# Two-block transformer on one core: convolution and decays made inside the projections, masks later, norms rearranged

## The reference

```python
# first block, delta rule branch
qkv = silu(centred_depthwise_conv(concatenate([q, k, v]), conv_w))   # 4 taps, 1536 channels
q, k = l2norm(heads(q)), l2norm(heads(k))
g = -exp(a_log) * softplus(a + dt_bias); beta = sigmoid(b)
o = gated_delta_rule(q, k, v, g, beta)                               # both directions

# every norm of the second block
h = rms_norm(x, norm_g) * (1.0 + scale) + shift                      # shift, scale, gate = silu(c) @ ada_w + ada_b

# second block, recurrence
q, f, i, g = split(h @ w_in)
log_f = logaddexp(log(lb), log1p(-lb) + log_sigmoid(f));  k = -expm1(log_f)
cum = cumsum(log_f)                                                  # in chunks
attn = einsum(q, k, exp(cum_t - cum_s)) for s <= t
o = attn @ i + (q * exp(cum)) @ state
```

## Time and profile before

| stretch | from, to us | PE busy | DVE busy | ACT busy | granted clock | GB/s |
|---|---|---|---|---|---|---|
| setup, to ScalarE's last copy and on | 0 to 15.3 | 0.59 | 0 | 1.92 | 1.00 | 282, then 401 |
| first norm | 15.3 to 23.2 | 7.63 | 4.37 | 3.51 | 1.00 | 388 |
| first projection, end of it | 73.0 to 81.0 | 7.22 | 2.33 | 0.39 | 0.59 | 88 |
| inputs stage, most of it | 81.0 to 111.0 | 21.25 | 20.10 | 20.44 | 0.83 | 336 |
| second projection, end | 1835.0 to 1851.6 | 15.73 | 1.62 | 1.84 | 1.00 | 253 |
| decay stage | 1851.6 to 1860.0 | 6.17 | 3.13 | 6.08 | 1.00 | 214 |
| decay stage, rest | 1860.0 to 1872.8 | 9.00 | 7.81 | 5.61 | 1.00 | 353 |
| scores, middle | 1880.0 to 1890.0 | 5.86 | 10.00 | 7.57 | 1.00 | 2 |
| scores, middle | 1890.0 to 1900.0 | 9.17 | 10.00 | 6.00 | 0.83 | 1 |

### The profile page before, as it was taken

The page is one execution under the profiler, slowest core; times in us unless marked ns, Lnnn a source line. Parts: engine busy times, 40 slices in busy tenths (PEclk is TensorE's granted clock), DMA queues, the critical chain, the costliest instruction groups (busy, mean ns, idle before and its releaser), DMA issues. The chain is left out here.

```text
span 2315.3 us, 27695 instructions
## 1 busy us (share of the span) xinstructions
PE 2050.6 (89%) x10647; PEld 1357.7 (59%) x10647; DVE 1398.4 (60%) x2485; ACT 618.2 (27%) x1042; POOL 504.8 (22%) x463
## 2 busy tenths in 40 slices
PE   7889998997997777877789888999999978899998
PEld 6679897774542222222238655666767866566684
DVE  5455563557888888655565564433757586533394
ACT  1411102422111111000020352333741061333472
POOL 1032000104443433344411170000101041100000
PEclk9889999999999999999999898999999999999999
DMA  5830655539999999999956303889995532698897
GB/s 200 308 124 1 212 192 185 218 107 411 394 421 422 421 422 421 422 421 417 422 208 208 126 2 138 358 353 361 385 388 203 198 110 75 232 368 349 351 418 275
DMA packets 142430, 650.96 MB, mean 281 GB/s; under 512 B 17975, under 2 KB 22735, under 8 KB 97083
## 3 DMA queue, kind: packets, MB, share of 16 engines
q1 hardware_dynamic: 94012, 354.09, 40.3%
q0 software_dynamic: 46336, 291.93, 30.9%
q10 hardware_dynamic: 1952, 3.18, 0.5%
HBM read 642.46 MB, written 16.85 MB: 285 GB/s over the span
## 5 line engine op out<-in xcount | busy, mean ns | idle before, releaser
L1842 PE MATMUL psum<-peer_uv_rows,peer_weight_diagonal 128*128 128x512 f32 x932 | 453.5, 615 | 109.4 <-DVE peer_weight_diagonal L1968 109.1
L1842 PEld LDWEIGHTS psum<-peer_uv_rows,peer_weight_diagonal 128*128 128x128 f32 x932 | 161.8, 190 | 391.8 <-DVE peer_weight_diagonal L1968 266.4
L1975 DVE SCALAR_TENSOR_TENSOR peer_uv_rows<-peer_uv_rows,peer_x 128x1024 f32<-128x1024 f32 x233 | 285.5, 1225 | 143.5 <-DMA peer_uv_rows<-peer_uv,peer_index 141.3
L1796 POOL DMA_INDIRECT peer_uv_rows<-peer_uv,peer_index x233 | 242.4, 1041 | 447.8 <-PE psum L1842 332.8
L147 DVE TENSOR_TENSOR moe_weight_parts<-weight_ring,moe_weight_parts 128x2048 fp32r<-128x2048 f32 x80 | 182.6, 2290 | 154.3 <-ACT moe_weight_parts L2891 153.9
L1875 ACT ACTIVATE peer_gelu<-peer_dots 128x1 f32<-128x1 f32 x256 | 51.5, 202 | 550.7 <-DVE peer_uv_rows L1975 499.1
L2891 ACT ACTIVATE moe_weight_parts<-weight_ring 128x2048 fp32r<-128x2048 f32 x80 | 152.1, 1911 | 36.7 <-DMA weight_ring<-moe_w 23.7
L153 PE MATMUL psum<-moe_weight_parts,moe_block_x_parts 128*128 128x512 f32 x352 | 142.9, 406 | 9.9 <-DVE moe_block_x_parts L147 5.3
L3010 POOL DMA_INDIRECT h_t<-moe_tokens,moe_block_tokens x30 | 35.1, 1170 | 500.4 <-PE psum L2709 410.8
L154 PE MATMUL psum<-moe_weight_parts,moe_block_x_parts 128*128 128x512 f32 x352 | 139.6, 397 | 0.0
L155 PE MATMUL psum<-moe_weight_parts,moe_block_x_parts 128*128 128x512 f32 x352 | 139.4, 396 | 0.0
(11 more groups left out here) (568 smaller groups left out, 3893.7 us busy)
## 6 DMA issues: line engine op xcount, KB each, us to landing
weight_ring<-moe_w SPq DMA_DIRECT2D x76, 2048.0 KB, 10.1
weight_ring<-ada_w SPq DMA_DIRECT2D x24, 2048.0 KB, 9.1
moe_weight_ring_end<-moe_w SPq DMA_DIRECT2D x20, 2048.0 KB, 12.6
weight_ring<-w_in SPq DMA_DIRECT2D x17, 2048.0 KB, 9.6
weight_ring<-hgrn_w_in SPq DMA_DIRECT2D x8, 2048.0 KB, 8.9
moe_results<-moe_block_out POOLq DMA_DIRECT2D x26, 512.0 KB, 9.0
weight_ring<-nsa_w_in SPq DMA_DIRECT2D x5, 2048.0 KB, 9.3
weight_ring<-peer_wq SPq DMA_DIRECT2D x4, 2048.0 KB, 8.0
```

What stands on the lines that cost most here:

```text
L1796: nc.gpsimd.indirect_dma_start(buffer(t), None, S.dram["peer_uv"], bass.IndirectOffsetOnAxis(ap=experts[:, t:t + 1], axis=0)).then_inc(row ...
L1842: last = nc.tensor.matmul(S.ps[:, 2 * a + c, :], diag[:, t % 4, :], v_rows(t)[:, c * BANK:(c + 1) * BANK], start=(i == 0), stop=(i == PICK ...
L1975: nc.vector.scalar_tensor_tensor(u_rows(t), u_rows(t), 1.0, x2[:, t // PICKS, :], ALU.mult, ALU.mult, accum_out=dots[:, t:t + 1]).then_inc ...
```

## The change

- Setup: SyncE waits only for x. The masks are loaded in the inputs stage, and so is the wait for the gate biases. The flip matrix is no longer loaded, VectorE makes it in the sparse attention.
- First projection: a class `Convolution` makes taps, SiLU and squares of q and k beside the units. The inputs stage begins with the sums of squares and v's SiLU; the six conditioning blocks come after.
- Norms with conditioning: shift and gain are made on GpSimd; VectorE evicts by column; no filler products ahead of a router, whose products wait column by column.
- Recurrence: f is projected first. A class `Decays` makes sigmoids (ScalarE), affine and floor (GpSimd), one logarithm, and the running sum as 16 scans (VectorE) beside the projection. `hgrn_decays` goes. Its three conditioning blocks are put between TensorE's levels of `hgrn_scores`, with one bank instead of two; the levels' ring is six banks; ScalarE makes the two last exponentials after level 3.

```diff
 @block.sync   # setup
                 S.w.load(sp, 1)
-                sp.dma_start(S.cst[:, C_LU:C_W], D_["cst"][:, C_LU:C_W]).then_inc(masks_in, 16)
-                S.w.load(sp, SLOTS)
                 sp.wait_ge(x_in, 16)
-                sp.wait_ge(masks_in, 16)
...
 # Conditioning.tensor
-            if i >= 2:
-                pe.wait_ge(self.moved, i - 1)
+            ahead = len(set(self.banks))
+            if i >= ahead:
+                pe.wait_ge(self.moved, i - ahead + 1)
...
 # norm_stage
+            @block.gpsimd
+            def _(pool):
+                if ada is not None:
+                    nc.gpsimd.tensor_tensor(mod[:, :], S.ada_cols[:, ada, :], S.col[:, COL_ADA + ada * 24:COL_ADA + ada * 24 + 2 * KD], ALU.add).then_inc(modulated, 1)
...
-                if ada is not None:
-                    link(nc.vector.tensor_tensor(mod[:, :], S.ada_cols[:, ada, :], S.col[:, COL_ADA + ada * 24:COL_ADA + ada * 24 + 2 * KD], ALU.add))
...
+                        for k in range(4):
+                            nc.vector.tensor_scalar(S.hT[:, k, a * P:(a + 1) * P], S.ps[:, 2 * a, k * P:(k + 1) * P],
+                                                    gain[:, k:k + 1], shift[:, k:k + 1], ALU.mult, ALU.add).then_inc(moved, 1)
...
-                    if work is None:
+                    if work is None and router is None:
                         idle_products(S, 6, 2)
...
-                            if k == 0:
-                                pe.wait_ge(moved, a + 1)
+                            if k < 4:
+                                pe.wait_ge(moved, 4 * a + k + 1)
...
+class Convolution:
+    AT = {0: (0,), 1: (1,), 4: (2, 3), 5: (4,), 6: (5,)}
...
+    def unit(self, dve, u):
+        dve.wait_ge(self.padded, 2)
+        dve.wait_ge(self.moved[u % 2], u // 2 + 1)
+        for tap in range(4):
+            for c in (2 * u, 2 * u + 1):
...
+    def scalar(self, act, i):
+        half = {4: 0, 7: 1}.get(i)
...
+        act.activation(part[:, :, :], part[:, :, :], ACT.Silu).then_inc(self.activated, 1)
...
+        act.activation(self.sq[:, 4 * half:4 * half + 4, :], part[:, :, :], ACT.Square).then_inc(self.squared, 1)
...
 # deltanet_inputs, TensorE
+                for half in range(2):
+                    for bank in range(2 * half, 2 * half + 2):
+                        last = nc.tensor.matmul(S.ps[:, bank, :], S.cst[:, C_ONES:C_ONES + P],
...
                 pe.wait_ge(cond_made, 1)
-                work.tensor(pe, 0, 3)
+                pe.wait_ge(S.bias_in, 4 * 16)
+                work.tensor(pe, 0, 2)
...
+                work.tensor(pe, 2, 6)
...
 # nsa_attention
+                nc.vector.tensor_copy(flip, ident[:, ::-1]).then_inc(flip_made, 1)
...
+                pe.wait_ge(flip_made, 1)
...
+class Decays:
+    SCANS = {8: 3, 9: 3, 10: 3, 11: 3, 12: 2, 13: 2}
...
+    def scalar(self, act, i):
...
+        if i == 7:
+            act.wait_ge(self.floored, 4)
+            logs = self.f[:, :, :].rearrange("p h t -> p (h t)")
+            act.activation(logs, logs, ACT.Ln).then_inc(self.logged, 1)
+
+    def gpsimd(self, pool):
+        nc, f, kT, lb = self.nc, self.f, self.kT, self.lb
+        pool.wait_ge(self.bounds, 2)
+        for i in range(4):
+            pool.wait_ge(self.kept, i + 1)
+            for h in (2 * i, 2 * i + 1):
+                nc.gpsimd.tensor_scalar(f[:, h, :], f[:, h, :], lb[:, 1, h:h + 1], lb[:, 0, h:h + 1], ALU.mult, ALU.add).then_inc(self.affine, 1)
+            pool.wait_ge(self.affine, 2 * i + 2)
+            pair = f[:, 2 * i:2 * i + 2, :].rearrange("p h t -> p (h t)")
+            nc.gpsimd.tensor_scalar(pair, pair, F_FLOOR, None, ALU.max).then_inc(self.floored, 1)
+            pool.wait_ge(self.forgotten, i + 1)
+            for h in (2 * i, 2 * i + 1):
+                nc.gpsimd.tensor_scalar(kT[:, h, :], kT[:, h, :], lb[:, 1, h:h + 1], None, ALU.mult)
+
+    def vector(self, dve, i):
...
+            if (h, a) == (0, 0):
+                dve.wait_ge(self.logged, 1)
...
+            nc.vector.tensor_tensor_scan(self.cum[:, h, part], S.cst[:, C_ONES:C_ONES + P], self.f[:, h, part], 0.0, ALU.mult, ALU.add)
...
 # hgrn_scores
+        work = Conditioning(S, st, ada_slots(3, 0, 1, 2), (6, 6), 7)
+        RING = 6
...
                     act.activation(flat(fs[n % 3]), flat(fs[n % 3]), ACT.Exp, scale=-1.0).then_inc(exped, 1)
-                act.activation(qe, cum[:, :, P:T], ACT.Exp).then_inc(begun, 1)
...
+                    if n == 3:
+                        act.activation(qe, cum[:, :, P:T], ACT.Exp).then_inc(begun, 1)
...
+                work.scalar(act, 0, 3)
...
+                nc.gpsimd.memset(flat(qs[1]), 0.0).then_inc(cleared, 1)
...
                     for b in range(4):
-                        if n >= 2:
-                            pe.wait_ge(kept, 4 * (n - 2) + b + 1)
+                        if 4 * n + b >= RING:
+                            pe.wait_ge(kept, 4 * n + b - RING + 1)
...
+                    if 3 <= n < 6:
+                        work.tensor(pe, n - 3, n - 2)
```

278 lines of the change are left out of this document (125 added, 153 removed).

## The result

The changed kernel takes 2295.47 us (median of 4 runs, 2291.59 to 2295.95); the kernel before, in all runs beside it, 2316.75. The ratio is 0.991, with a 95% interval of 0.9898 to 0.9922: 21.3 us faster. Its profiled execution has a span of 2294.0 us (2315.3 before); TensorE is busy for 2033.3 us of it (89%), VectorE for 1390.1, ScalarE 614.9, GpSimd 537.1. The forecast was 2298.5, with a range of 2292 to 2307.

A forecast was written before the change was run, and what follows sets the result against it. Bounds were taken stage by stage: masks in the opening, TensorE in both projections, VectorE in the scores. Terms -4.95 + 1.0 + 0.5 - 4.7 - 0.2 + 0.3 - 21.2 + 10.8 = -18.45 gave 2298.5 us, range 2292 to 2307.

The forecast's parts named there:

- Rival (d): Opening: the wait only moves to a weight block or x, no gain of 5, 2303.5 us; chance 0.05.
- First projection: Convolution's 19 us on VectorE beside the first projection stay covered, 3.6 us of cover left; cost 0.
- Inputs stage: Inputs stage of the delta rule: sums first, then late weight loads and a slow last block; +1.0 us, bounds -1 to +2.5.
- Delta rule: Delta rule starts with a lower clock: +0.5 us (0 to 1).
- Norms ahead of the routers: Norms before the two routers: earlier mean, no filler products, router products column by column; -2.35 us each, -4.7.
- The earlier end is passed on: After the routers' norms: the gain is kept, because the experts' weights are only issued after routing.
- Recurrence, projection: Second projection: GpSimd's 21 us and VectorE's sixteen scans are covered beside TensorE; cost 0.
- (b): Second projection: VectorE bounds it, shut out by GpSimd's instructions; +7 us, 2305.6 us; chance 0.07.
- (e): Second projection: scans wait for GpSimd's 20 instructions, later splits queue behind; slower than before, 2329 us at 4.0 apiece; chance 0.03.
- Scores: Scores stage: block 1 waits for row 0 behind ScalarE's last exponential; +10.8 us, bounds +8.9 to +13.
- Rival (c): Scores and routers: the clock stays low, levels take 7.1 us, routers give nothing; near 2310 us; chance 0.06.
- Rival (a): Scores: the moved blocks hide in TensorE's 2 us gaps per level, +10.8 falls away, 2287.7 us; chance 0.07.

The follow-up runs named there:

- experiment 9: Changed kernel, but VectorE makes the first tap of every tile and every scan four times: 2316.43 us, ratio 1.0003.
- experiment 8: Changed kernel, but the four filler products ahead of a router's products stay: 2299.84 us, ratio 0.9922.
- experiment 11: Kernel before with the recurrence's part alone, and the flip made on VectorE: 2307.9 us, ratio 0.997.
- experiment 3: Changed kernel, but in the inputs stage TensorE multiplies conditioning block 0 before the four sums over squares: 2295.03 us, ratio 0.9901.

## Why the prediction was right, and where it wasn't

**Opening** (-4.95): right, -5.20, and 5.7 with an interval of 2.8 to 7.4 by itself. The step that failed is the arrival of the second block (19.6 instead of 17.7). Rival (d) needed it to matter; it doesn't, since norm and projection together take 63.5 us as before.

**First projection** (0): right, but the cover was 2.8 us and not 3.6, and it is the only one (experiment 9). The sentence that every further microsecond would count was measured: beyond the cover each one did, and the low clock behind the wait added 2.7. I had taken ScalarE's and TensorE's idle places as signs of room; the engine to add up was VectorE, which is full from 19.6 us to the last tap.

**Inputs stage** (+1.0): right to a tenth in the profiled execution, and the tenth is luck. The first slot came 8.2 us after the stage's start (9.1 in the sum), the three loads took 19.9 us (18.1), and from the last landing to the next stage it was 5.3 us (6.2): -0.9, +1.8 and -0.9. The first two loads behind an idle queue took 8.7 us for the one and 5.7 more for the other, where I had 1.9 and twice 5.4. Also, by the window in rows 8 the clock rose at 84.6, not 84.3. Executions of kernels with this stage span 32.3 to 34.1. What the sum did get is the order of things: slot, three loads, last block. What I drew from it was too weak: not that the convolution's removal is worth nothing because loads are next, but that the new order of the sums made the loads late. The same stage took 30.8 us with the taps in it and conditioning first, and 29.6 without them in a better order.

**Delta rule** (+0.5): wrong in sign, -1.1 and -1.9 in two executions. It did start at the low clock, as forecast (its first 32 products with the triangle took 6.10 us instead of 5.45), but the granted clock of the 10 us from +40 on was 0.66 where it had been 0.56 before. Five traces with the old inputs stage ahead of it have 127.7 to 128.1 us, eight with the new one 125.7 to 128.0, in the mean 1.2 less. The step that failed is the price of the low start: it is paid, but a later low stretch is shorter, and the forecast had only the first. Why the clock goes that way wasn't tested.

**Norms ahead of the routers** (-2.35 each): right, -2.31 and -2.32, and the fillers are 1.2 and 2.1 of it by experiment 8. The rows that I named give 2.14 (1410.7 instead of 1412.84); the other 0.2 had no row. The first of these norms scatters, too: 8.9 to 9.6 us in nine traces without fillers and 11.2 to 11.7 in three of the old norm. **Norms ahead of a projection** (-0.1 each): -1.0 and -0.6 in the trace, of which the first is one execution's clock. Whether 0.1 was right can't be told beside a scatter of 1.

**"The earlier end is passed on"**: right for the first expert stage, 331.9 to 333.0 us in all traces but two (333.1 in the kernel before, 334.4 in the changed kernel's first). Wrong for the second, and this is the part of the sum that was missing: +1.6. A block of results must be stored before ScalarE may evict the next one. First the kernel before, then the changed one:

```profile
2189.22 1.03 ACT L2932 ACTIVATE moe_block_out<-psum 128x1024 f32<-128x1024 f32 x1 [5.30 <-DMA moe_results<-moe_block_out]
```

```profile
2167.50 1.03 ACT L2968 ACTIVATE moe_block_out<-psum 128x1024 f32<-128x1024 f32 x1 [6.85 <-DMA moe_results<-moe_block_out]
```

TensorE's idle time behind it grew by as much, from 1.89 to 3.44 us. The stage takes 333.2 to 333.7 in the three traces with the old recurrence and 334.6 to 336.9 in the ten with the new one, experiment 11 among them, whatever the rest. So it comes with the recurrence's part. It can be narrowed down to one store: the one that this eviction waits for, issued 202.7 to 203.9 us after the stage's start, lands 4.0 to 4.1 us later in the three traces and 5.3 to 5.7 in the ten, though the stores and loads around it are issued at the same places. Why it lands later, I don't know; that stays open.

**Flip** (+0.3): the copy takes 0.23. The attention stage takes 71.8 to 72.1 us in the ten traces with it and 73.0, 71.5 and 71.9 in the three without, so neither the 0.3 nor the -1.1 of the table can be told from scatter.

**Recurrence, projection** (0): right, 93.1 us in every trace but that of experiment 9. GpSimd was under-sized (31.7 us instead of 21), because it is slowed while VectorE splits: two scalings took 1.82 us beside an idle VectorE and 5.60 beside its splits. The logarithm's lead of 10.6 us covered it, so (b) and (e) had the contention right and the consequence wrong. Two scalings with two column operands, for which (e) had no row, took 1.07. VectorE's first split, beside GpSimd's own, took 4.33 us, the last ones 2.29. By the Trainium skill ("GPSIMD Engine Reference", section 8) the two share their interfaces to the SBUF and contend where a VectorE instruction runs in a 2-port perf mode or has two inputs there. The trace agrees for the splits, which have two. VectorE's high parts, with one input, were stretched as well, 3.37 us at 1755.28 against 1.22 elsewhere; in which mode they ran the trace doesn't tell. The threshold for a scan was 0.8 us and not 1.0: the cover of 5.5 us in experiment 9, over 12 scans, is 0.46 each on top of 0.32.

**Decays** (-21.2): right. **Scores** (+10.8): +9.5. The mechanism was read from the code and rows 7 and held in every step: row 0 at +34.6 (34.7 forecast), a slow block 1 (3.35; I had 3.5), two fast levels, two turns. Mis-sized was level 5, 3.8 instead of 4.5, since the clock rose sooner. The clock behind the hole differs from trace to trace (0.84, 0.79, 0.54), which makes this stage 65.5 to 68.4 us long with its outputs; my bounds of 8.9 and 13 allow for that. Rival (c) didn't come: behind the slow block the levels ran in 3.82, 3.82 and 3.74 us. Rival (a) described what a better order can do: with the rows in between the term is +1.1.

**Sum.** -18.45 was forecast, -21.3 came out. The known terms have errors of -0.3 (opening), -1.6 (delta rule), -1.3 (scores), +1.6 (second expert stage); the rest, some -1.2, is in stages that the change doesn't touch or that scatter by as much. (The bounds of the terms add up to 2306.6 at the upper end, not 2306.3.) Whole times divide the gain in another way: opening 5.7, norms 5.9 and recurrence 7.1 us by themselves, and 2.3 to 3.6 lost when the convolution is moved back, together some 21 to 22. The forecast had 4.95, 4.9, 10.1 and -1.5 for them. The recurrence gave less than forecast (4.9 to 9.3 by its interval); for the convolution the intervals of the two kernels overlap. If both differences are real, the total came within 3 us of the forecast in part because they cancel, and that is luck. The stage lengths show only a part of either (+1.6 in the second expert stage, -1.2 in the delta rule); where the rest lies stays open.

## What to carry over

When work is moved beside other work, write down for each engine what its queue holds in order, and for each wait who moves the data that it waits for and what stands ahead of that. Both times here a copy of 0.3 us, put behind ScalarE's long chain, kept TensorE or a weight slot waiting for several us; moving that copy gave 8.5 us in the scores, and with a better order of the blocks 2.7 in the inputs stage.
A buffer more doesn't help when a later step of the same queue needs the same row, and an earlier first release doesn't help when the last load hangs on the third.
A stage length from one trace is good to a tenth where TensorE has no idle time (93.1 us for the second projection, each time), and to 2 us where the clock rises and falls (to 5 us for the attention's projection with its preparations, 106.1 to 111.6); look at the same stage in a second execution before giving it a cause.

## What was unexpected of the hardware

The clock makes equal programs differ by over a microsecond in a single norm. The windows of the first 4 us of the norm ahead of the attention show a granted clock of 0.59 in the short one (7.7 us) and 0.50 in the long one (8.8) of the changed kernel; what differs is whether it rises ahead of the transposes or behind them.

GpSimd slows by up to 3 times beside VectorE's splits (0.91 us for a scaling of 256 columns, 2.80 beside a split), and a split beside GpSimd by 1.9. Alone, a scaling of 256 columns with two column operands (multiply and add) took 0.54 us, less than one with a single operand.

A load of 2 MB with no other load under way took 8.1 to 9.4 us to land (32.24 to 40.34 and 81.68 to 90.43 in the changed kernel, 93.50 to 102.88 in experiment 3); in the inputs stage the ones issued behind it landed 5.3 to 6.3 us after each other, where their slot was free in time.

A scan over 128 columns costs hardly more than the custom instruction of that size in rows 3 (0.32): 0.40 us each, 0.32 from start to start.
